# Later modulation chunks, raw bank copies on ScalarE, and a reordered attention in a two-block transformer kernel

## The reference, cut to what is computed

```python
def reference(...):                       # D = 1024, 256 tokens, batch 1
    x = first_block(x, ...)               # attention and product-key experts
    return second_block(x, c, ctx, ...)   # two layers on x (latent) and ctx (context)

def first_block(h, ...):
    proj = rmsnorm(h, norm1_g) @ w_in     # q, k, v twice, two gates: 1024 -> 5120
    y_a = moba_attention(...) @ w_out_moba         # 8 heads, causal, ALiBi
    y_b = stick_breaking_attention(...) @ w_out_sb # 8 heads
    h = h + (sigmoid(gate_a) * y_a + sigmoid(gate_b) * y_b) @ w_mix_out
    return rmsnorm(h + peer_ffn(rmsnorm(h, norm2_g), ...), final_norm_g)

def peer_ffn(x, ...):                     # 8 heads, top 16 of 128 x 128 experts each
    u, v = expert_u[e_idx], expert_v[e_idx]        # 128 rows of 1024 each, per token
    return einsum(g * gelu(einsum(x, u)), v)

def second_block(x, c, ctx, ...):
    for i in range(2):
        # six shifts, scales and gates for x and for ctx out of silu(c) @ mod_w[i] + mod_b[i]
        a = modulate(rms_norm(h, norm_mix_g[i]), shift, scale)
        o = short_conv_mixer(a) if i == 0 else mla_mixer(a_ctx, a_lat)   # 16 heads in the latter
        h = h + g1 * o
        h = h + g2 * swiglu(modulate(rms_norm(h, norm_ffn_g[i]), ...), ...)   # hidden 2816
    # ctx gets its update in layer 0 only
```

## Time and profile before

| | us |
|---|---|
| median of 3 runs | 1945.71 |
| lowest, highest | 1941.71, 1948.63 |
| the profiled execution | 1930.46 |
| its span | 1928.7 |
| PE busy | 1722.7 (89%) |
| DVE busy | 1193.9 (62%) |
| ACT busy | 606.8 (31%) |
| POOL busy | 583.6 (30%) |
| moved by DMA | 515.93 MB, 268 GB/s in the mean |

### The profile page before, as it was taken

The page is one execution under the profiler, slowest core; times in us unless marked ns, Lnnn a source line. Parts: engine busy times, 40 slices in busy tenths (PEclk is TensorE's granted clock), DMA queues, the critical chain, the costliest instruction groups (busy, mean ns, idle before and its releaser), DMA issues.

```text
span 1928.7 us, 25422 instructions
## 1 busy us (share of the span) xinstructions
PE 1722.7 (89%) x10050; PEld 1338.9 (69%) x10050; DVE 1193.9 (62%) x2094; ACT 606.8 (31%) x915; POOL 583.6 (30%) x570
## 2 busy tenths in 40 slices
PE   6999899798879798998778868999999897889998
PEld 5776589675536365675546648989998543579998
DVE  4344255877697887678787576556542479535553
ACT  4446534211111212121211014235532123635532
POOL 0111100477667676566767640000000100000000
PEclk9999899899989999999889989999999999999999
DMA  7999954799999999999999983446553222035553
GB/s 263 320 330 317 335 200 139 289 408 410 408 393 409 409 397 409 409 408 408 408 409 409 406 338 128 157 130 194 179 195 99 70 74 77 1 103 181 179 191 109
DMA packets 222956, 515.93 MB, mean 268 GB/s; under 512 B 13244, under 2 KB 121996, under 8 KB 222860
## 3 DMA queue, kind: packets, MB, share of 16 engines
q0 software_dynamic: 86784, 318.80, 42.5%
q1 hardware_dynamic: 135728, 195.71, 29.7%
q10 hardware_dynamic: 348, 0.11, 0.0%
HBM read 513.53 MB, written 1.05 MB: 267 GB/s over the span
## 4 chain that ended last, share of the span: by engine, by line
PE 49%; DMA 22%; DVE 13%; POOL 7%; issue 4%; ACT 3%; ACTq 0%; DVEq 0%; SPq 0%; POOLq 0%
DMA more<-in_peer_v_dram,idx 15%; PE bank L842 10%; PE bank L845 10%; PE bank L843 9%; POOL more L741 7%; DMA more<-in_peer_u_dram,idx 4%; PE bank L796 4%; DVE more L2199 3%; PE bank L1138 2%; PE wide L1186 2%; DVE rstd L2271 2%; PE wide L952 2%; PE bank L1077 2%; DMA weights<-in_w_in_dram 1%; PE bank L836 1%
## 5 line engine op out<-in xcount | busy, mean ns | idle before, releaser
L1814 DVE TENSOR_TENSOR low_weights<-weights,high_weights 128x2048 fp32r<-128x2048 f32 x108 | 247.4, 2292 | 296.7 <-ACT high_weights L1482 296.1
L2199 DVE CUSTOM_DVE_ANT_0 more<-more,wide 128x1024 f32<-128x1024 f32 x256 | 311.0, 1219 | 143.1 <-DMA more<-in_peer_u_dram,idx 141.3
L842 PE MATMUL bank<-high_input,high_weights 128*128 128x256 f32 x1312 | 373.4, 285 | 17.6 <-DVE low_input L1863 8.2
L843 PE MATMUL bank<-high_input,low_weights 128*128 128x256 f32 x1344 | 377.8, 281 | 0.0
L845 PE MATMUL bank<-low_input,high_weights 128*128 128x256 f32 x1312 | 370.3, 282 | 0.0
L741 POOL DMA_INDIRECT more<-in_peer_u_dram,idx x256 | 285.4, 1115 | 246.4 <-DVE idx L2103 100.0
L1186 PE MATMUL wide<-more,rstd 128*128 128x512 f32 x476 | 250.7, 664 | 113.2 <-ACT rstd L1660 107.7
L1482 ACT ACTIVATE high_weights<-weights 128x2048 fp32r<-128x2048 f32 x108 | 206.8, 1916 | 306.7 <-DMA weights<-in_ffn_w_gate_dram 92.2
L741 POOL DMA_INDIRECT more<-in_peer_v_dram,idx x256 | 252.6, 987 | 105.2 <-issue 71.5
L842 PEld LDWEIGHTS bank<-high_input,high_weights 128*128 128x128 f32 x1312 | 248.2, 189 | 25.9 <-issue 21.6
L1186 PEld LDWEIGHTS wide<-more,rstd 128*128 128x128 f32 x476 | 94.9, 208 | 241.0 <-ACT rstd L1660 136.3
(11 more groups left out here) (251 smaller groups left out, 2356.6 us busy)
## 6 DMA issues: line engine op xcount, KB each, us to landing
weights<-in_ffn_w_down_dram SPq DMA_DIRECT2D x33, 1024.0 KB, 5.0
weights<-in_ffn_w_gate_dram SPq DMA_DIRECT2D x30, 1024.0 KB, 5.4
weights<-in_ffn_w_up_dram SPq DMA_DIRECT2D x30, 1024.0 KB, 5.4
weights<-in_conv_w_in_dram SPq DMA_DIRECT2D x24, 1024.0 KB, 7.8
weights<-in_w_in_dram SPq DMA_DIRECT2D x20, 1024.0 KB, 9.6
nrm<-in_mod_w_dram POOLq DMA_DIRECT2D x16, 1024.0 KB, 7.5
sq<-in_mod_w_dram POOLq DMA_DIRECT2D x16, 1024.0 KB, 7.1
h_ctx<-in_mod_w_dram POOLq DMA_DIRECT2D x16, 1024.0 KB, 7.4
```

What stands on the lines that cost most here:

```text
L842: first = nc.tensor.matmul(out, cut(high), hi, start=start, stop=False, **more_args)
L843: nc.tensor.matmul(out, cut(w_lo[b]), hi, start=False, stop=False, **more_args)
L1814: return nc.vector.tensor_tensor(out, a, b, op)
L2199: nc.vector.tensor_tensor_reduce(u, u, wide[0][:, :], 1.0, 0.0, ALU.mult, ALU.add, dots[:, n % 16:n % 16 + 1]).then_inc(s_dot, 1)
```

## The change

- **Start.** The identity, the two halves of x and the remaining constants are loaded by separate transfers with their own semaphores; the repeated gain rows are loaded by one transfer each instead of one per copy (16 small loads instead of 24). The vectors' transposes and copies stand behind the sum for norm 1; the first weights' high part stands ahead of the norm's root.
- **Modulation.** Chunks 40 to 47 use two other buffers, loaded once the first attention has ended. Chunk 40 stands behind the output products, 41 behind the context's transposes, 42 to 44 between the `mix` products, 45 before `peer_q`, 46 and 47 in it. The second layer's modulation is finished in the gather loop at step 24.
- **Scores.** ScalarE copies the last five groups of expert scores after the first exponential.
- **Gather loop.** The second early weight tile gets its low part after the last row, and the first tile's sums are taken at step 247 instead of 253.
- **Latents.** ScalarE copies the two key-value latent banks raw; VectorE scales them in place. The same is done for the last key pair, whose reciprocal and scaling are four pieces in attention steps 1 to 4; the last rope turn goes ahead of that pair.
- **Attention.** Transposes go ahead of the pair product, and the transposed probabilities get a third buffer. The first two `mla_out` products are done in two parts, the first seven of eight input tiles ahead of (or right behind) the last pair product.
- **Store.** The result is transposed and stored in four quarters, the first two as soon as the first two banks of the last product are added.

The diff, cut to its core (declarations, the lists that only repeat the new order and unchanged lines are left out):

```diff
...
+LATE_MODS = list(range(40, 48))
+LATE_BUFFER = dict(zip(LATE_MODS, [0, 1, 0, 1, 0, 1, 0, 0]))
+def late_landed(j):
+    return 16 * sum(1 for m in LATE_MODS if m <= j and LATE_BUFFER[m] == LATE_BUFFER[j])
...
-    return [FIRST - 1 + 2 * s, FIRST + 2 * s]
+    return [j for j in (FIRST - 1 + 2 * s, FIRST + 2 * s) if j < LATE_MODS[0]]
...
+    if _s == 5:
+        PEER.append(("mod_turn", MOD_QUADS - 1))
...
-MIXES = [("turn_ctx", _g) for _g in range(4)] + [("mix", 0), ("mixnorm_ctx", 0), ("mix", 1), ("mix", 2), ("mix", 3)]
+MIXES = [("turn_ctx", _g) for _g in range(4)] + mod_turns(41) + [("mix", 0), ("mixnorm_ctx", 0), ("mix", 1), ("mix", 2), ("mix", 3)]
...
-LOW_AT = [248, 252]
+LOW_AT = [248]
...
+MODULATE_AT = 24
...
-FIRST_SUMS = SLOTS_P - 3
+FIRST_SUMS = SLOTS_P - 9
...
-        mprob_t = view(more, 16384, 2, 4, T)
+        mprob_t = [view(more, 16384, 4, T), view(more, 17408, 4, T), view(big, 8320, 4, T)]
...
-            sp.dma_start(x_tok, w["x"][0].rearrange("(a p) d -> p a d", p=P)).then_inc(s_tokens, 16)
-            sp.dma_start(consts[:, :], consts_dram[:, 0:CCOLS["end"]]).then_inc(s_tokens, 16)
+            sp.dma_start(ident, consts_dram[:, 0:P]).then_inc(s_ident, 16)
+            for t in range(2):
+                sp.dma_start(x_tok[:, t, :], w["x"][0][t * P:t * P + P, :]).then_inc(s_tokens[t], 16)
+            sp.dma_start(consts[:, P:CCOLS["end"]], consts_dram[:, P:CCOLS["end"]]).then_inc(s_consts, 16)
...
-            wait_all_emptied(sp, "turn_out", 4)
-            sp.dma_start(out_dram[0].rearrange("(a p) d -> p a d", p=P), out_tok).then_inc(s_out, 16)
-            sp.wait_ge(s_out, 16)
-        N_VECTORS = 16 * 24
+            for g in range(4):
+                half, t = g // 2, g % 2
+                wait_emptied(sp, "turn_out", g)
+                sp.dma_start(out_dram[0][t * P:t * P + P, 512 * half:512 * half + 512],
+                             out_tok[:, t, 512 * half:512 * half + 512]).then_inc(s_out, 16)
+            sp.wait_ge(s_out, 64)
+        N_VECTORS = 16 * 16
...
-                if j >= 3:
+                late = j >= LATE_MODS[0]
+                if j == LATE_MODS[0]:
+                    wait_emptied(pool, "pair", HALVES // 2 - 1)
+                if late:
+                    for m in LATE_MODS:
+                        if m < j and LATE_BUFFER[m] == LATE_BUFFER[j]:
+                            last = m
+                    if j >= LATE_MODS[2]:
+                        pool.wait_ge(s_mod_used, last + 1)
+                elif j >= 3:
...
-                nc.gpsimd.dma_start(mod_w[j % 3], mv[:, 2 * part:2 * part + 2, at:at + D]).then_inc(m_landed[j % 3], 16)
+                src = mv[:, 2 * part:2 * part + 2, at:at + D]
+                if late:
+                    nc.gpsimd.dma_start(late_w[LATE_BUFFER[j]], src).then_inc(late_landed_at[LATE_BUFFER[j]], 16)
+                else:
+                    nc.gpsimd.dma_start(mod_w[j % 3], src).then_inc(m_landed[j % 3], 16)
...
-                pe.wait_ge(m_landed[j % 3], 16 * (j // 3 + 1))
+                if j >= LATE_MODS[0]:
+                    buffer = late_w[LATE_BUFFER[j]]
+                    pe.wait_ge(late_landed_at[LATE_BUFFER[j]], late_landed(j))
+                else:
+                    buffer = mod_w[j % 3]
+                    pe.wait_ge(m_landed[j % 3], 16 * (j // 3 + 1))
...
-                                              mod_w[j % 3][:, k, 512 * half:512 * half + 512],
+                                              buffer[:, k, 512 * half:512 * half + 512],
...
-            pe.wait_ge(s_tokens, 32)
-            turn_tokens("turn_x", x_tok)
+            pe.wait_ge(s_ident, 16)
+            for t in range(2):
+                pe.wait_ge(s_tokens[t], 16)
+                for g in range(4):
+                    if t == 0:
+                        wait_free(pe, "turn_x", g)
+                    b = bank_of("turn_x", g)
+                    for a in range(2):
+                        mm = nc.tensor.transpose(bank[b][:, 256 * a + 128 * t:256 * a + 128 * t + 128],
+                                                 x_tok[:, t, (2 * g + a) * P:(2 * g + a + 1) * P], ident)
+                    if t == 1:
+                        mm.then_inc(full[b], 1)
+            pe.wait_ge(s_consts, 16)
+            norm_stream("norm1")
...
-            norm_stream("norm1")
...
-                    for j in LAST_MODS[2 * n + s]:
-                        mods(j)
-            mod_turn(MOD_QUADS - 1)
+            mods(40)
...
+            mods(41)
...
+                if s < 3:
+                    mods(42 + s)
...
+            mods(45)
...
+                if s in (2, 3):
+                    mods(44 + s)
+                if s == 5:
+                    mod_turn(MOD_QUADS - 1)
...
-            rope_turn(QUADS - 1)
+                if n == KV_FIRST:
+                    rope_turn(QUADS - 1)
+            def mla_out_part(s, ks):
+                wt = ring[slot_of("mla_out", s)].rearrange("p (k n) -> p k n", k=KD)
+                if ks[0] == 0:
+                    wait_weights(pe, "mla_out", s)
+                    wait_free(pe, "mla_out", s)
+                b = bank[bank_of("mla_out", s)]
+                for m in range(2):
+                    for k in ks:
+                        mm = nc.tensor.matmul(b[:, m * T:(m + 1) * T], wt[:, k, m * P:(m + 1) * P], o_mla[:, k, :],
+                                              start=(m == k == 0), stop=(k == KD - 1), skip_group_check=True)
+                        if m == 0 and k == (0 if s == 0 else KD - 1):
+                            opens("mla_out", s, mm)
+                if ks[-1] == KD - 1:
+                    mm.then_inc(full[bank_of("mla_out", s)], 1)
...
+                if 0 <= s - MLAG < MH:
+                    n = s - MLAG
+                    pe.wait_ge(s_prob_v, HEADS + n + 1)
+                    for half in range(2):
+                        turns("mla_attention", MATT.index(("turn", 2 * n + half)),
+                              [(256 * a + 128 * t, mprob[n % 3][:, t, (2 * half + a) * P:(2 * half + a + 1) * P])
+                               for a in range(2) for t in range(2)])
+                if s == MH + MLAG:
+                    wait_emptied(pe, "mla_attention", MATT.index(("pair", 6)))
+                    mla_out_part(0, range(7))
...
-                            mm = nc.tensor.matmul(b[lo:lo + MV, 0:T], vmla[:, a, MV * n:MV * n + MV], mprob_t[:, n % 2, a, :],
+                            mm = nc.tensor.matmul(b[lo:lo + MV, 0:T], vmla[:, a, MV * n:MV * n + MV], mprob_t[n % 3][:, a, :],
...
-                if 0 <= s - MLAG < MH:
-                    n = s - MLAG
-                    pe.wait_ge(s_prob_v, HEADS + n + 1)
-                    for half in range(2):
-                        turns("mla_attention", MATT.index(("turn", 2 * n + half)),
-                              [(256 * a + 128 * t, mprob[n % 3][:, t, (2 * half + a) * P:(2 * half + a + 1) * P])
-                               for a in range(2) for t in range(2)])
-            wait_all_emptied(pe, "mla_attention", len(MATT))
-            products("mla_out", lambda k: o_mla[:, k, :], 4)
+            mla_out_part(1, range(7))
+            wait_emptied(pe, "mla_attention", MATT.index(("pair", 7)))
+            for s in range(2):
+                mla_out_part(s, [7])
+            for s in range(2, 4):
+                product("mla_out", lambda k: o_mla[:, k, :], KD, 0, s)
...
-            wait_all_emptied(pe, "down_1", 4)
...
-                turns("turn_out", g, [(P * a, h_lat[:, 4 * (g % 2) + a, (g // 2) * P:(g // 2) * P + P]) for a in range(4)])
+                half, t = g // 2, g % 2
+                for b in range(2 * half, 2 * half + 2):
+                    wait_emptied(pe, "down_1", b)
+                turns("turn_out", g, [(P * a, h_lat[:, 4 * half + a, t * P:t * P + P]) for a in range(4)])
...
+            high("qkv", 0)
+            act.wait_ge(s_consts, 16)
+            root("norm1", D)
...
-            high("qkv", 0)
-            root("norm1", D)
...
-                for j in LAST_MODS[n]:
-                    mod_rows(j)
...
-            leave_modulation(MOD_QUADS - 1)
...
+            mod_rows(41)
...
+                if g == 1:
+                    mod_rows(43)
...
+            mod_rows(45)
...
-            for g in range(3, 8):
-                scores(g)
+                if s == 3:
+                    mod_rows(47)
+                if s == 5:
+                    leave_modulation(MOD_QUADS - 1)
...
+            for g in range(3, 8):
+                scores(g)
...
+            for m in range(2):
+                leave("mla_in", m, kvlat[:, m, :])
...
+                if n == MH // 2 - 1:
+                    b = bank_of("kv", 2 * n)
+                    nc.scalar.activation(kcat[0:NOPE, 2 * n, :], bank[b][0:NOPE, :], ACT.Copy)
+                    nc.scalar.activation(kcat[NOPE:P, 2 * n + 1, :], bank[b][NOPE:P, :], ACT.Copy).then_inc(free[b], 1)
...
-                if s >= MLAG + 2 and s % 2 == 0:
```

(40 more changed lines are left out.)

32 lines of the change are left out of this document (17 added, 15 removed).

## The result

| | before | after |
|---|---|---|
| median of 4 runs each, us | 1944.91 | 1923.20 |
| lowest, highest | 1941.71, 1948.63 | 1917.21, 1926.99 |
| the profiled execution | 1930.46 | 1926.99 |
| its span | 1928.7 | 1924.9 |

The ratio of after to before is 0.9885, 95% interval 0.9853 to 0.9917: 22.4 us less. The forecast was 28.9 us less, 1916.8 us, with its own range of 1909 to 1925. The time is inside this range, but nearer to rival D's 1924 than to the forecast.

The account below looks back on a forecast made before the run. Early stage and gather loop DMA-bound, the rest TensorE-bound, with short latency chains at the joints. Terms 3.3 + 8.2 + 6 + 2 + 3 + 3.7 + 2.7 = 28.9 us, off 1945.71, gave 1916.8 us; range 1909 to 1925.

Parts of the forecast that it names:

- rival D: Early stage stays byte-bound, mix products wait for mix 2's weights: parts 1 and 2 give 4, not 11.5; 1924; chance 0.14.
- part 3: Gather loop's end: sums before row 248, full clock, split hidden, row 255's vector landing near 1151; gain 6 us (3 to 7.5).
- 4: root of mla_in to q_ones' reciprocal: Latent banks: raw copies free the bank, so the second query product needn't wait; gain 2 us (0.5 to 4).
- 5: from there to the end of the maximum that the forecast names: Last key pair: fifth head's maximum ends near 1642.5 instead of 1645.2; gain 3 us (0 to 4).
- 6: from there to the last norm's reciprocal: Attention order and third buffer: waits before pairs go, out products fill late waits; gain 3.7 us (0 to 6).
- 7: last residuals to the end: End: earlier transposes and a last store of 256 KB landing in about 2.4 us; gain 2.7 us (2 to 3.3).
- Part 1: Start: fewer small loads, vectors behind the norm; reciprocal near 17.9 instead of 21.04; gain 3.3 us (2 to 4.5).
- the gain isn't eaten by the DMA-bound beats: Start: the queue is idle between 30 and 33 us, so later loads shift too and the 3.3 us gain survives.
- Part 2: Late modulation chunks: 15.6 us earlier, less TensorE work and contention (1.9 and 1.5); gain 8.2 us (3 to 10).
- The allowance of 2.5 us for up_1's slot: Attention's end: ring slot of up_1's first weights opens 5.3 us later, pushing the last squares; 2.5 us off the gain.
- rival A: Contention and low clock take more: terms at low ends give 10.5 us, 1935; typically about 16, 1930; chance 0.20.
- C: Slower: late chunks land as slowly as gathered rows; 20 us landings expose 28 us, the whole gain; chance 0.04.

Follow-up runs that it names:

- b_again: The kernel before once more, no edit, traced again in set 2; first to last gather 785.9 us (that kernel's time in set 2: 1934.59 us).
- c_before: The kernel before, no edit, traced in set 3 on the same chip as the changed kernel; 1934.90 us, loop 786.0 us.
- e1: The changed kernel again, no edit, in set 1; 1918.91 us against 1948.01 for the kernel before, ratio 0.9854.
- c_after: The changed kernel, no edit, in set 3 on the same chip as the kernel before; 1910.76 us, ratio 0.9872, loop 786.2 us.
- e5: The kernel before with nothing but the late modulation chunks; 1933.62 us against 1934.59, ratio 0.9994.
- e6: The changed kernel with ScalarE's high parts of peer_q 2 and 6 moved behind work the first gather needs; 1907.62 us, ratio to before 0.9842.
- e8: The changed kernel with those two splits moved, plus chunk 47 in its own buffer and chunks 46, 47 loaded together earlier; 1903.05 us, ratio to before 0.9837.
- e9: The changed kernel with the attention undone (last key pair, order, two buffers, unsplit out products); 1919.11 us, ratio to before 0.9925.

## Why the prediction came out as it did

The time fell in the range: 22.4 us less against 28.9. All of the shortfall is in parts 1 and 2. Parts 3 to 7 add up to the forecast (17.5 against 17.4 us), with errors that cancel: part 3 has 1.1 less, the others 1.2 more. By parts, from traces (mean of before, b_again and c_before against after, e1 and c_after, first gather; behind it before, b_again, c_before, e5 against after, e1, c_after, e6, e8):

| step | forecast | measured |
|---|---|---|
| 1, 2: first gather | 11.5 | 4.7 |
| the loop, first to last gather, same set | 0 | -0.2 |
| 3: last context residual to final reciprocal | 6 | 4.9 |
| 4: root of mla_in to q_ones' reciprocal | 2 | 2.4 |
| 5: from there to the end of the maximum that the forecast names | 3 | 3.8 |
| 6: from there to the last norm's reciprocal | 3.7 | 3.4 |
| 7: last residuals to the end | 2.7 | 3.0 |
| sum | 28.9 | 22.0 |

The first row is the uncertain one, for the early stage varies by 7 us: the c pair alone has 8.1 there and 24.1 in all.

**Part 1** was mis-sized at its own mark. The reciprocal moved by 2.3 us in the first pair and by 1.7 in the mean of fourteen traces, not by 3.3: the sums ended at 16.6, the root at 18.4 and the low part at 18.6, and only then came the reciprocal, at 18.75 and not near 17.9; and the 21.04 of the trace before is a little later than that start is in the mean (20.8). The step "the gain isn't eaten by the DMA-bound beats" is borne out up to 126 us and open behind that.

**Part 2**: the 15.6 us were nearly right (15.0, of which some 0.8 are the start's), and so was the cost of the chunks on TensorE. The failed term is the contention. I wrote "between 0 and 4.3 us each" and took 1.9 and 1.5, by halving a transfer; it was 2.5 and 3.2, about a whole transfer of the added megabyte (2.6 us at 400 GB/s, the prediction's own figure). Another 1.2 us stand in no term of the sum. I had read in the earlier trace rows that both landings were on the path already and had concluded that a later landing counts in full; it did, and e6 shows the way out that this reading offers: not to shorten the landing but to take the first scores from behind it.

**Part 3**: sums ahead of row 248 and full clock came as described. The failed step is the landing of row 255's vector. I let it come 1.4 us sooner because its issue would take 0.94 instead of 2.75. The issue did; the landing did not (9.97 against 9.95 us from the issue's start, 9.92 in both c_before and c_after, 9.91 to 9.97 in all fourteen traces). The time from issue to landing is the same too, first in c_before, then in c_after:

```profile
more<-in_peer_v_dram,idx POOLq DMA_INDIRECT x1, 9.8
```
```profile
more<-in_peer_v_dram,idx POOLq DMA_INDIRECT x1, 9.8
```

What sets it is the queue. When row 255's gather is issued, seven earlier ones have still to land, and they land 1.27 us apart (half a megabyte each, 413 GB/s by my estimate), row 255's as the last, in both kernels. A shorter issue can't overtake them. So it caps the gain at 4.9. The split of 2.3 is hidden as said (1165.49 to 1167.8, the tile's addition at 1168.14).
By the Trainium skill (SBUF — State Buffer, Who interferes with whom) the shared port pair is an exclusive lock, and a VectorE instruction with two SBUF inputs, as the split is, contends with a GpSimd instruction that reads SBUF, not with one that only writes it. The issue's 2.75 us beside the split and 0.94 without it agree with a lock; by which port it works no run here shows. That the landing would follow was my addition, and it didn't.

**Parts 4 to 7** came within 0.8 us each; the fifth and sixth together are 7.2 us against 6.7, and e9 puts them at 8.7 in the same marks. The maximum that the prediction calls the fifth head's (it ends at 1645.2 in the trace before) is the sixth's if heads are counted from one. The last of the four stores landed 2.2 us after its issue, near the 2.4 of the forecast; the single one before took 4.0. Two heads take 7.35 us (forecast 7.45). The allowance of 2.5 us for up_1's slot was too high, if anything.

**Rivals.** D named the right size, 4 us for parts 1 and 2 (measured 4.7), and its 1924 is nearer to the 1923.20 than the forecast's 1916.8. But it got there by luck, for neither of its reasons holds: the start's shift is whole at 126 us, and the mix products did not wait for mix 2. They started when forecast, and the loss came behind them, by the contention of rival A. C needed landings of 20 us; the late loads took 7.3 in the median. The forecast of the loop's length held in the same set, though my own test of it ("it would be wrong if the gather loop's length moved by more than 5 us") would have condemned it by the first pair of traces: a mark must be compared in one set of runs. Of its other signs, pair 7's copy was to come near 223.5 and the first gather near 344; they came at 228.1 and 352.8. In the feed-forward stages the clock is 1.00 before and after.

Rival A's "each wait over 3 us was followed by a slow stretch" is true of its two rows, but not of this trace. Here is the kernel before at two other waits, the slow one after the shorter:

```profile
1029.32 3.51 PE L1186 MATMUL wide<-more,rstd 128*128 128x512 f32 x4 [2.49 <-ACT rstd L1660]
...
1133.31 1.98 PE L1186 MATMUL wide<-more,rstd 128*128 128x512 f32 x4 [3.73 <-ACT rstd L1660]
```

## What to carry to other kernels

When a transfer is added to a stretch with idle queues, look in each engine's queue for splits and copies that wait for a landing with urgent work behind them. Price the delay at the whole time of the added transfer, not at half of it, or first move the urgent work ahead. A gain of 2 us ahead of a stage whose end varies by 7 us can't be read at that end: follow it through marks inside the stage, in many traces. Before a stage that the change doesn't touch is explained from two traces, trace the old kernel again beside the new one.
